# Two 256 x 1024 x 1024 products of each layer of block 1 done as seven half-size products, their weight sums by accumulating transfers, and the decay rows by broadcast transfers

## What is computed

```
proj = x @ w_in                       # 256 x 1024 by 1024 x 5136, split into
q, k, v, z_attn, z_ssm, xbc, dt_raw
attn = sliding_window_attention(q, k, v, sinks) * silu(z_attn)
xbc  = silu(causal_depthwise_conv(xbc, conv_w, conv_b))   # xs, B, C
dt   = softplus(dt_raw + dt_bias);  a = -exp(a_log)
a_cs = cumsum(dt * a)                 # per head, within a chunk of 128 tokens
y    = (C B^T * exp(a_cs_i - a_cs_j), lower triangle) @ (xs*dt)  +  state terms
y    = y + xs * d_skip
ssm  = rmsnorm(y * silu(z_ssm))
out  = concat(attn, ssm) @ w_out      # 256 x 2048 by 2048 x 1024
x    = layer_norm(sqrt(2) * x + out)
```

## Time and profile before

| what | value |
|---|---|
| median of 3 runs | 1929.64 us (1929.03 to 1929.65) |
| the profiled execution, whole | 1927.62 us |
| its span, first to last instruction | 1925.8 us |
| PE busy | 1566.3 us (81%) |
| DVE / ACT / POOL busy | 681.8 / 304.8 / 13.0 us |
| moved by transfers | 554 MB |

### The profile page before, as it was taken

One profiled execution on the slowest core, in us unless ns is written; L12 is line 12 of the kernel. 1 busy time (PEld: TensorE's weight loads), 2 busy tenths in 40 slices (PEclk: granted clock), 3 DMA queues, 4 the chain that ended last, 5 costly groups with the idle time before them and its releaser, 6 DMA issues.

```text
span 1925.8 us, 20585 instructions
## 1 busy us (share of the span) xinstructions
PE 1566.3 (81%) x8874; PEld 892.2 (46%) x8874; DVE 681.8 (35%) x1395; ACT 304.8 (16%) x804; POOL 13.0 (1%) x39
## 2 busy tenths in 40 slices
PE   9999999999999999766555656655665556799999
PEld 7775567755667845222212222212222122357886
DVE  3663455634486864311111111101111111144533
ACT  1343313432122102000000000000000000213220
POOL 0000000000000000000000000000000000000000
PEclk9999999999999999978778888788887888899999
DMA  9851376414243456999999999999999999954300
GB/s 378 280 151 46 107 275 219 131 53 165 97 171 136 176 218 264 429 430 430 432 431 428 433 428 430 434 428 431 429 429 432 432 431 428 375 197 171 127 10 22
DMA packets 87779, 554.35 MB, mean 288 GB/s; under 512 B 4512, under 2 KB 11424, under 8 KB 74112
## 3 DMA queue, kind: packets, MB, share of 16 engines
q1 hardware_dynamic: 86544, 548.81, 71.0%
q0 software_dynamic: 1136, 4.10, 0.6%
HBM read 551.85 MB, written 1.05 MB: 287 GB/s over the span
## 4 chain that ended last, share of the span: by engine, by line
PE 60%; DMA 35%; DVE 4%; ACT 1%; issue 0%; POOL 0%; SPq 0%; DVEq 0%; ACTq 0%; POOLq 0%
PE bank L679 27%; DMA ring<-in_w 22%; DMA arena<-in_w 12%; PE bank L1174 8%; PE bank L706 7%; PE bank L688 6%; PE bank L1202 3%; PE bank L667 3%; PE bank L1487 1%; PE bank L878 1%; PE bank L811 1%; PE bank L791 1%; DVE arena L2427 0%; PE bank L1145 0%; PE bank L1225 0%
## 5 line engine op out<-in xcount | busy, mean ns | idle before, releaser
L1174 PE MATMUL bank<-ring,arena 128*32 128x512 f32 x1216 | 283.4, 726 | 147.1 <-DMA arena<-in_w 96.7
L1174 PE MATMUL bank<-arena 128*32 128x512 f32 x832 | 228.9, 722 | 101.1 <-DMA ring<-in_w 101.1
L679 PE MATMUL bank<-ring,arena 128*128 128x512 f32 (+3 forms) x744 | 304.5, 560 | 0.8 <-ACT tmp L1543 0.8
L679 PE MATMUL bank<-arena,ring 128*128 128x256 f32 (+1 forms) x1632 | 291.9, 337 | 0.5 <-DVE arena L3106 0.5
L679 PEld LDWEIGHTS bank<-arena,ring 128*128 128x128 f32 x1632 | 256.5, 191 | 30.6 <-issue 7.5
L679 PEld LDWEIGHTS bank<-ring,arena 128*128 128x128 f32 x744 | 138.5, 191 | 129.9 <-issue 118.6
L1174 PEld LDWEIGHTS bank<-ring,arena 128*32 128x32 f32 x1216 | 71.4, 131 | 266.6 <-issue 266.6
L1202 PE MATMUL bank<-ring,arena 128*32 128x512 f32 x576 | 126.4, 681 | 27.8 <-DMA arena<-in_w 18.8
L1174 PEld LDWEIGHTS bank<-arena 128*32 128x32 f32 x832 | 56.3, 130 | 186.2 <-issue 186.0
L706 PE MATMUL bank<-ring,arena 128*128 128x512 f32 (+1 forms) x320 | 127.4, 555 | 1.6 <-DVE arena L2029 0.8
L1202 PE MATMUL bank<-arena 128*32 128x512 f32 x384 | 102.7, 696 | 20.8 <-DMA ring<-in_w 20.8
(11 more groups left out here) (396 smaller groups left out, 1477.1 us busy)
## 6 DMA issues: line engine op xcount, KB each, us to landing
ring<-in_w SPq DMA_DIRECT2D x53, 4096.0 KB, 31.6
arena<-in_w SPq DMA_DIRECT2D x35, 4096.0 KB, 37.7
ring<-in_w_in SPq DMA_DIRECT2D x40, 2048.0 KB, 8.2
ring<-in_w_mod SPq DMA_DIRECT2D x6, 2048.0 KB, 12.5
ring<-in_w_out SPq DMA_DIRECT2D x6, 2048.0 KB, 7.9
arena<-in_w SPq DMA_DIRECT2D x6, 2048.0 KB, 10.5
ring<-in_w SPq DMA_DIRECT2D x6, 2048.0 KB, 12.5
ring<-in_w_out SPq DMA_DIRECT2D x16, 512.0 KB, 9.2
```

Of the source, the lines that this page charges most:

```text
L679: i = te.matmul(ps, lhsT, rhs, start=n0 + k == 0, stop=n0 + k == n - 1)
L1174: m = te.matmul(ps[32 * j:32 * j + 32, :], LM.xg[:, f, 128 * k + 32 * j:128 * k + 32 * j + 32], vs[j][:, 512 * (k % 2):512 * (k % 2) + 512 ...
```

## The change

1. **Seven products.** With the tokens split in two (rows), and each weight matrix in four quarters (half of the inputs, half of the columns), each of the two products is made from seven products of 128 tokens x 512 inputs x 512 columns (four matmuls each, P1 to P7) where there were eight. Four sums of token tiles are needed first; DVE makes them (`layer_token_sums`, four TENSOR_TENSORs of 128x512), and DVE combines the seven results (`layer_gate_sums`, `layer_out_sums`) through two scratch tiles, `part` and `part1`. For the output, DVE also adds sqrt(2) h there, in two instructions per tile.
2. **Weight sums by transfers.** The host gives the two matrices as quarters (`w_quads`). SP loads three slots for each matrix where it loaded two (the third, "T", again holds quarters 2 and 3), in one piece each, so a layer has 20 loads. POOL then issues four accumulating transfers of 1 MB for each matrix (`accum_op=ALU.add`), two of them from DRAM and two from one part of SBUF to another.
3. **Decay rows.** One step early in the convolutions PE makes the cumulated decays as rows (`acsT`, two matmuls with 128 columns), ACT copies them out, POOL stores them to DRAM and later loads them back to all partitions, 1 MB for each token tile. ACT's Relu reads these rows. The eight "mb" turns of a layer are gone.
4. **Banks and places.** P1 to P7 use banks 4 to 7 in rotation; `banks.width = 4` is set ahead of the gate's steps, not behind. The accumulators of `out_ssm` hold the state-space half alone. Since the rotation is another one, the second layer's first "vd" group (v and dt of tokens 0 to 127) lands in bank0, before it was bank3; the transposes of tokens 128 to 255 go to bank2 and bank3 in both.

The core of the diff:

```
@@ sync_program
-            turn, in_turn = [5], list(range(NR))
+            turn, in_turn = [1], list(range(NR))
...
+                load_quadrants(("zs", ly, 0), 0, 0)
+                load_quadrants(("zs", ly, 1), 0, 2)
+                load_quadrants(("T", "zs", ly), 0, 2)
+                load_quadrants(("oa", ly, 0), 1, 0)
+                load_quadrants(("T", "oa", ly), 1, 2)
+                load_quadrants(("oa", ly, 1), 1, 2)
@@ tensor_program
+                def times(k, x, w):
+                    ps = fresh("P", name, ly, k, b=4 + ((k - 1) if name == "zs" else k + 6) % 4)
+                    product(ps[:, :], [(x[:, c, :], w[:, c, :]) for c in range(4)]).then_inc(*t.done("mm", "P", name, ly, k))
...
                 banks.width = 4
+                yield from layer_seven("zs", ly, hT)
                 ready(*[("ev", "pv", ly, n) for n in range(4)])
...
+                yield from layer_seven("oa", ly, L1.zaT)
...
-                        for q in range(2):
-                            t.wait_ge(*at.of("ev", "acs", ly))
-                            turn(("mb", ly, tt, g, q),
-                                 [(128 * i, bc(L1.acs[:, tt, 8 * g + 4 * q + i:8 * g + 4 * q + i + 1], 128)) for i in range(4)])
-                            yield
+                        yield
+                        yield
@@ vector_program
+                to_part(X, 4, ALU.add).then_inc(*v.done("ev", "P", "oa", ly, 4))
+                yield
+                to_part(Y, 5, ALU.subtract, flip=True).then_inc(*v.step())
+                residual(0, 1, 3, Y, ALU.subtract)
+                yield
+                to_part(X, 6, ALU.add).then_inc(*v.done("ev", "P", "oa", ly, 6))
+                residual(1, 1, 5, X, ALU.subtract)
@@ gpsimd_program
+                def load_rows(tt, free):
+                    ready(("rows", "stored", ly), free)
+                    ge.dma_start(L1.rows[tt].rearrange("p g n -> p (g n)"), bcast(rows_out[ly, tt], 2048)
+                                 ).then_inc(*loaded[tt].inc())
+                for name, k in (("zs", 1), ("zs", 3), ("zs", 2), ("oa", 1), ("zs", 4), ("oa", 2), ("oa", 3), ("oa", 4)):
+                    if (name, k) == ("zs", 2):
+                        load_rows(0, ("mm", "sc", ly, 3, 1))
+                    if (name, k) == ("oa", 2):
+                        load_rows(1, ("mm", "pT", ly, 3, 1, 1))
...
+                    ge.dma_start(dst, src, accum_op=ALU.add).then_inc(*summed[k - 1].inc())
```

More of the change, by code:

```diff
@@ L238, in program @@
         ada_c_sem = sem("ada_c_loaded")
+        rows_stored_sem = sem("cumulated_rows_stored")
+        rows_sem = [sem(f"cumulated_rows{tt}_loaded") for tt in range(2)]
+        rows_out = nc.dram_tensor("cumulated_rows", (2, 2, 2048), F32, kind="Internal").ap()
+        summed_sem = [sem(f"weights_summed{k}") for k in range(4)]
         h_sem = [sem(f"h{tt}_loaded") for tt in range(2)]
@@ L307, in program @@
             lng, lnb = ar(22848, 1024), ar(23872, 1024)
+            sums = [ar(22848 + 512 * k, 4, 128) for k in range(4)]
+            part, part1 = ar(22336, 512), ar(6144, 512)
             y = ar(17464, 2, 1024)
@@ L310, in program @@
             Btok = ar(20544, 256)
+            rows = [ar(2048, 16, 128), ar(15408, 16, 128)]
             Mt = ar(20800, 8, 128)
@@ L757, in layer_proj @@
                     for i in range(4):
+                        if g + i == 0:
+                            ps = fresh("acsT", ly)
+                            t.wait_ge(*at.of("adt", ly))
+                            for tt in range(2):
+                                m = te.matmul(ps[0:16, 128 * tt:128 * tt + 128], L1.adt[:, tt, :], tri[:, :], start=True, stop=True)
+                            m.then_inc(*t.done("mm", "acsT", ly))
                         feat(("cv", ly, 4 * g + i), hT, weights(("cv", ly, g)), 128 * i)
@@ L1643, in layer_ssm @@
                     yield
+                ready(("rows", "stored", ly))
                 out_copy(("B", ly), L1.Btok, bank("B", ly)[:, 0:256])
@@ new lines, in layer_proj, with layer_token_sums @@
+                yield from layer_gate_sums(ly)
+                yield from layer_out_sums(ly)
+            def layer_token_sums(name, ly, xT):
+                lo, hi = slice(0, 128), slice(128, 256)
+                s1, s2, s3, s4 = L1.sums
+                behind()
+                if name == "oa":
+                    ready(("mm", "P", "zs", ly, 6))
+                ve.tensor_tensor(s1, xT[:, 0:4, hi], xT[:, 4:8, hi], ALU.subtract).then_inc(*v.step())
+                ve.tensor_tensor(s3, xT[:, 0:4, lo], xT[:, 0:4, hi], ALU.subtract).then_inc(*v.step())
+                behind()
+                ve.tensor_tensor(s2, s1, xT[:, 0:4, lo], ALU.subtract).then_inc(*v.step())
+                behind()
+                ve.tensor_tensor(s4, xT[:, 4:8, lo], s2, ALU.add).then_inc(*v.done("S", name, ly))
@@ new lines, in layer_gate_sums, with to_part, half, gate @@
+            def layer_gate_sums(ly):
+                X, Y = L1.part, L1.part1
+                def to_part(dst, k, scale, other, op=ALU.add):
+                    ready(("mm", "P", "zs", ly, k))
+                    behind()
+                    return ve.scalar_tensor_tensor(dst, bank("P", "zs", ly, k)[:, :], scale, other, ALU.mult, op)
+                def half(tt, g, k, other, op):
+                    to_part(L1.zs[:, tt, 512 * g:512 * g + 512], k, 0.5, other, op).then_inc(*v.done("ev", "P", "zs", ly, k))
+                    v.also("half", "zs", ly, tt, g)
+                def gate(tt, g):
+                    gated(("zs", ly, tt, g), L1.zs[:, tt, 512 * g:512 * g + 512], 512)
+                yield
+                yield
+                ready(("ev", "P", "zs", ly, 1))
+                half(0, 0, 2, X, ALU.add)
+                yield
+                to_part(X, 4, 0.5, X).then_inc(*v.done("ev", "P", "zs", ly, 4))
+                yield
+                ready(("mm", "sc", ly, 3, 1))
+                to_part(Y, 5, -0.5, X).then_inc(*v.step())
+                half(0, 1, 3, Y, ALU.subtract)
+                gate(0, 0)
+                yield
+                to_part(X, 6, 0.5, X).then_inc(*v.done("ev", "P", "zs", ly, 6))
+                half(1, 1, 5, X, ALU.subtract)
+                yield
+                layer_token_sums("oa", ly, L1.zaT)
+                yield
+                gate(0, 1)
+                yield
+                half(1, 0, 7, X, ALU.add)
+                gate(1, 1)
+                yield
@@ L2327, in norm_sums @@
                 v.wait_ge(*at.of("mm", "o", ly, tt, n))
-                ve.scalar_tensor_tensor(hv, hv, ALPHA, P[4 + 2 * tt + n][:, :], ALU.mult, ALU.add
-                                        ).then_inc(*v.done("ev", "o", ly, tt, n))
+                ve.tensor_tensor(hv, hv, bank("o", ly, tt, n)[:, :], ALU.add
+                                 ).then_inc(*v.done("ev", "o", ly, tt, n))
                 behind()
```

169 lines of the change are left out of this document (117 added, 52 removed).

## The result

The changed kernel takes 1937.33 us (1936.31 to 1939.24, 7 runs), the kernel before 1929.03 us (1926.31 to 1931.71, 7 runs). The ratio is 1.0043 with an interval of 1.0033 to 1.0053: 8.3 us slower, where 1928.8 and no change were forecast. The profiled execution has a span of 1936.0 us.

What follows compares the result with a forecast made beforehand. Block 1 was taken as a chain of PE work: -19.6 us of work, + 2 x 10.8 of new waits, -0.8 and -2.0 of old ones gave -0.8, so 1928.8 us; 8-in-10 range 1919 to 1945, own range 1924 to 1935.

Steps and rivals of the forecast that it cites:

- PE's work: Each layer loses two products and eight turns, 10.3 us, and gains two `acsT` matmuls, 0.49: net -9.8 us a layer.
- The new waits: PE waits 3.8 us at the first decay tile, 0.9 third, 4.4 at the output's P7, 1.7 for banks: 10.8 a layer.
- The old waits: The first layer's 0.83 us wait at a gate tile and the 2.0 us for DVE's L2103 go: -0.8 and -2.0.
- DVE in the convolutions: The first four sums, 2.75 us, stand where DVE has idle time: 0 for PE, at most 1 us a layer.
- Transfers: POOL's ten in a row, 8 us per accumulating megabyte against 9.9 us available: PE does not wait, 0.
- (a): First decay tile: four token sums on DVE delay its second half, so PE waits 3.8 us a layer.
- (c): P7 of the output needs P3 out of bank5, which DVE empties late: PE waits 4.4 us a layer.
- three signs of being wrong: PE waiting for DMA at L689, a "yb" wait under 2 us, or PE's work gain not 9.8 us a layer.
- signs of being right: DVE waits of 3 to 5 us at L910 and L689, 0.8 and 0.9 at L677, out products near 214.5 us.
- orders bind more: Rival: DVE's sums and transfer load delay hand-overs, 1 us more at each of three waits: +6, 1935 us; chance 0.14.
- Cover holds: Rival: ACT works ahead, chains at first decay tile and output's P7 half as long: -9, 1920.6 us; chance 0.18.
- transfers late: Rival: accumulating transfers above 9.9 us each hold up P4 and P7: 1946 at 11 us, over 2020 at 16; chance 0.18.

Runs made afterwards that it cites:

- e4: Changed kernel with decays computed in place one tile ahead, the four sums one step later and the output's seventh product in bank 6: 1907.59 us, 0.9893 of before.
- e5: Changed kernel with idle products filling its two long waits of each layer, 4 and 5 of 128x512: 1928.83 us, 0.9996 of the kernel before.
- e10: Kernel before with decay rows by broadcast transfers, decays in place one tile ahead, still eight products: 1919.97 us, 0.9954 of the kernel before.
- e11: The kernel of e4 run again, beside e10 on the same chip: 1910.32 us, 0.9898 of the kernel before.

## Why the prediction was wrong

**PE's work, -9.8 us a layer: right.** It can be read off in e4, where no long wait is left. The experts' first matmul starts at 743.43 us there and at 760.03 in the kernel before, 16.6 earlier. The sum: -19.6, the old waits -2.8, the waits for a bank +3.0 as measured, four smaller waits +0.8 (0.63 for 0.40 twice, 0.20 for none, 0.87 for 0.78) and the first products +1.8 (the open point above) make -16.8.

**The new waits, 10.8 us a layer: right**, 10.6 measured, each within 0.2 us. Adding up the chains of ACT and DVE from the earlier trace rows worked. My bounds of a tenth each way were wider than needed.

**The old waits, -0.8 and -2.0: right.** Neither is in the trace. In the second layer the bank wait of 0.88 us (L2072) takes the place of one of 0.78.

**DVE in the convolutions, 0: nearly right.** One wait of 0.2 us in the second layer.

**Transfers, 0: right in the sum, wrong in the working.** 13 us each and not 8, but overlapping and not in a row.

**The step that failed: the sum ended at PE's idle time.** It took a wait to cost its own length. Here PE's records behind the four long waits are stretched by 9.4 us, because the clock is granted at half. That is a term that belongs to both waits, (a) and (c), in each layer, and it was missing; with it the forecast would have been 1928.8 + 9.4 = 1938, against 1937.3. Filling the waits with idle products gave 8.5 us back, and a wait put into the kernel before brought the half clock there. The granted clock is a column of the earlier trace rows, where it stands at 0.82 in the experts' stretch, with its many pauses; I did not ask what lowered it there. The Trainium skill (TensorE: Matmul & The Clock Gate, "HAM oscillation — how this bites in real kernels") describes this mechanism for waits for transfers: the engine drops to half its rate in a wait and starts the next piece cold, and the advice is to restructure so that it stays warm. The rows of e5 and e4 agree, with 1.00 behind the waits that were filled or taken away. Beside the forecast's own waits of 3.8 and 4.4 us it called for a term that the sum did not have.

None of the prediction's three signs of being wrong appeared, since none of them looks at how long the work behind a wait takes. The one that would have told is among the signs of being right: the out products were due near 214.5 us and started at 219.65, 4.5 us of it the clock's.

The rival "orders bind more" gave 1935, the nearest in time, for a reason that was not the one found. "Cover holds" and "transfers late" did not occur. That 1937.3 lies within 1919 to 1945 is luck: the room above 1935 was there for late transfers.

## What to carry to other kernels

Where the sum of a change comes out near zero because saved work and new waits cancel, the waits are the dearer part: price TensorE's long waits at their length plus the half-speed work behind them, here 1.5 to 4.4 us for each. Work taken from an engine is also cover taken from its partners, so first move the partners' chain (here: compute in place, a tile ahead, another bank) and then take the work out; the same seven products cost 10 us before that and gave 10 us after it. When a wait can't be removed, idle products that just fill it give the clock's share back.

## What the runs showed of the hardware

Whether the clock falls behind a wait is not the same each time. In the 13 profiles, from 90 to 720 us, all 20 waits of PE of 2.67 to 4.69 us had the half clock behind them; of 15 waits of 1.96 to 1.98 us seven had it; of 15 of 1.54 to 1.58 us one; of 68 of 0.63 to 0.93 us none. The wait of 1.97 us at L1010 is in every kernel, and was followed by half speed in the kernel before but not in e10 (PE in order of time and the clock, first before, then e10):

```profile
675.56 1.79 PE L1010 MATMUL bank<-arena 128*128 128x128 f32 x8 [1.97 <-DVE arena L2037]
...
676.00:679.00 3.00, 3.00 (x13) 0.50 0.00 0
```

```profile
666.94 1.16 PE L1017 MATMUL bank<-arena 128*128 128x128 f32 x8 [1.97 <-DVE arena L2053]
...
667.00:670.00 3.00, 3.00 (x16) 1.00 0.00 0
```

That alone is about 1.7 us between one profile and another. These are profiles of different kernels; e4 and e11, the same kernel, both had the half clock there, so that no run shows it come and go within one kernel at this wait. The wait of the earlier trace rows, 1.96 us, had 1.00 behind it in both kernels that have it.

An accumulating transfer of 1 MB took 13 us from issue to landing beside other loads, one of 8 KB 3.1 us. It lengthened the loads beside it (7.9 to 17.1 us for 2 MB) without costing the kernel anything.
